# A stage multiplies its successor's first two projection lots before the border

## The chip, the cores and the metric

One core of a Trainium2 chip runs one program: two blocks, one after the other, each a row of stages. The metric is the device time of one execution in microseconds; the kernel before takes 3568.51 us at the median of three runs.

## The reference, cut to what matters

Each block computes, from the modulated and normed tokens `h` (256 context and 512 grid tokens, width 1024), projections through one large matrix, runs two recurrent mixers on them, gates and merges the two results and projects back:

```python
z = jnp.matmul(h, w_in)                                # all projections
oa, ob = mixer_a(z), mixer_b(z)                        # chunked scans, both directions
ya = rmsnorm(oa, ...) * silu(ag); yb = rmsnorm(ob, ...) * silu(bg)
gates = sigmoid(mg + b_gate)                           # mg is one of the projections
merged = gates[..., :D] * (ya @ w_a) + gates[..., D:] * (yb @ w_b)
out = merged @ w_o
```

In the first block mixer a is a gated linear attention (4 heads) and mixer b a gated delta network (4 heads). In the second, mixer a is HGRN2 (8 heads) and mixer b a state space mixer (8 groups), and a product-key expert layer follows. All is float32.

## The kernel before, in words

**Stages.** A stage is a function that gives each engine its own instruction stream inside one block; all engines meet in a barrier at its end, and PSUM and semaphores pass from one stage to the next only there. The four borders of this document lie between `gla_pairs` and `gdn_heads` (first block, mixers a and b), `gdn_heads` and `merge`, `gated_heads` and `ssd_groups` (second block, mixers a and b), `ssd_groups` and `merge`.

**Tiles and lots.** A mixer stage projects its weights tile by tile (128 output channels, 1024x128, 512 KB). SyncE loads tile n into one of two slots of the ring once `low_ready` says that the tile two before it was split; ScalarE casts it to a rounded high part (`high(n)`, after the matmuls that still read this slot: `lot_done`), and VectorE subtracts to get the low part (`low(n)`). TensorE multiplies a tile with the tokens in lots of 384 or 512 columns: a lot is 8 units (one for each 128 of the width), a unit is `product3`, three matmuls (low by high, high by low, high by high; lines 366 to 368). Lots go to PSUM banks 6 and 7 in turn, and ScalarE evicts them (`evict`, semaphore `evicted`).

**Fills.** The lots of a stage are one generator, `projection()`; `fill(count)` issues the next `count` units between the other TensorE work of a head, in an order written out by hand (`FILL`, `SLOT`). Each mixer works a head or group ahead, so in its last head or group the generator has run dry and the fills issue nothing. `onward` lists tiles of the successor: the stage loads and splits its successor's first two tiles (`ready` = 2 tells the successor so), but multiplies nothing with them.

**The ends.** `gla_pairs` handles two pairs of heads (steps `at` = 1 to 14 each): key rows (line 594) at step 9, state updates (608) at 8 and 10, output products (lines 638 and 641) at step 12, the sums of squares (648) at step 14, then ScalarE's rstd and VectorE's last product. In `gdn_heads` each head ends with six passes over the chunks: TensorE, VectorE, TensorE, VectorE, TensorE, VectorE, each waiting for the other (lines 1237, 1250, 1261 on TensorE; 1646, 1654, 1662 on VectorE), with the output products at 1269 and 1270 and `squares` (1189). `gated_heads` is built like `gla_pairs` with 8 heads (output products 3007 and 3010, squares 2962); in the last head bank 6 also turns the step sizes (line 3017), which ScalarE copies out (3147, `dt_kept`). `ssd_groups` has 8 steps in a group: ScalarE exponents, VectorE product (3826), TensorE output products (3554, 3555); the norm (3505) ends the last group, and then the stage waits for its store to DRAM.

**The starts.** `gdn_heads` forms running sums (1192), then `fill(24)` multiplies three lots; ScalarE evicts lot 0 once the convolution weights and the pair mask have landed (`const_in`), and VectorE begins with `low(2)` (line 1461) and the convolution of the queries. `ssd_groups` forms sums, then `fill(72)` multiplies all nine lots of the first group, the first four of 384 columns. `merge` multiplies 16 gate tiles (8 units of 512 columns each) in order into banks 0 to 7, the sigmoid evicts each (`gate_ready`); tile i+2 is split while tile i+1 is multiplied. Beside it, it loads the branch weights (0.5 MB in the first block, 1.5 MB in the second) and, in the second block, the mixer's result `yz` piece by piece.

## Time and profile before

| | |
|---|---|
| median of three runs | 3568.51 us (3567.75 to 3574.23) |
| profiled execution | 3568.87 us, span 3566.7 us, 48214 instructions |
| TensorE busy | 3304.1 us, 93% |
| VectorE, ScalarE, GpSimd busy | 2540.0, 1617.3, 547.7 us |
| `gla_pairs`' last output products to `gdn_heads`' first matmul | 259.9 to 270.0 us |
| `gdn_heads`' last output to merge's first matmul | 614.9 to 620.0 us |
| `gated_heads`' last output to `ssd_groups`' first lot | 1322.1 to 1335.4 us |
| `ssd_groups`' last output to merge's first matmul | 1921.4 to 1935.9 us |

The span is the time from the first to the last instruction that the profiler saw; the execution's own time lies 2.2 us above it. The lower four rows are the stretches around the borders in the timeline. Times in the timeline are microseconds from the start of the span. The engines are PE (TensorE), PEld (its weight loads), DVE (VectorE), ACT (ScalarE), POOL (GpSimd) and SP (SyncE); an engine name with a q is its instruction queue.

### The profile page before, as it was taken

The numbers are of one execution on the slowest core, as the hardware profiler recorded it, in microseconds if no ns is written. First come the engines' busy times: TensorE is split into PE (matmuls) and PEld (weight loads), VectorE is DVE, ScalarE is ACT, GpSimd is POOL, SyncE is SP. The second block draws the span as 40 slices with busy tenths as digits, with TensorE's granted clock in tenths as the row PEclk, the third lists the DMA queues.
The fourth block names the chain that finished last, engine by engine and source line by source line (L and its number), as shares of the span: only waits on it lengthen the run. The fifth ranks groups of instructions, "written<-read, shape, count | busy, mean of one in ns | idle before, by whom it ended". The sixth has DMA issues, their size and how long they took to land. (4 is left out here: it accounts for less than half of the span.)

```text
span 3566.7 us, 48214 instructions
## 1 busy us (share of the span) xinstructions
PE 3304.1 (93%) x18404; PEld 2877.1 (81%) x18404; DVE 2540.0 (71%) x4360; ACT 1617.3 (45%) x2671; POOL 547.7 (15%) x365
## 2 busy tenths in 40 slices
PE   7988998997999979999997998999998999999997
PEld 3867987875889878777875886899997788999996
DVE  2646886254877875887884435699995887888887
ACT  4433342325555543665564423433564444444444
POOL 0211010000433420000000000455100111222220
PEclk9989999998999989999998999999999999999999
DMA  5101110342111111111112324334467998999994
GB/s 222 36 24 54 31 36 20 117 166 95 46 50 48 48 30 55 48 54 48 60 48 94 108 89 193 140 134 150 149 216 274 359 355 329 354 354 354 345 355 158
DMA packets 152468, 521.20 MB, mean 146 GB/s; under 512 B 19136, under 2 KB 66096, under 8 KB 132400
## 3 DMA queue, kind: packets, MB, share of 16 engines
q1 hardware_dynamic: 133808, 383.90, 29.9%
q0 software_dynamic: 18432, 134.23, 10.2%
q8 instruction: 147, 2.41, 0.3%
q14 instruction: 81, 0.66, 0.1%
HBM read 474.01 MB, written 44.06 MB: 145 GB/s over the span
## 5 line engine op out<-in xcount | busy, mean ns | idle before, releaser
L366 PE MATMUL ps<-hT_high,ring_twin 128*128 128x384 f32 (+1 forms) x1768 | 691.3, 391 | 64.5 <-DVE ring_twin L3188 32.5
L368 PE MATMUL ps<-hT_high,ring_twin 128*128 128x384 f32 (+1 forms) x1768 | 649.9, 368 | 0.0
L367 PE MATMUL ps<-hT_low,ring_twin 128*128 128x384 f32 (+1 forms) x1696 | 621.5, 366 | 0.0
L366 PEld LDWEIGHTS ps<-hT_high,ring_twin 128*128 128x128 f32 x1768 | 343.8, 194 | 121.8 <-DVE ring_twin L3188 38.2
L368 PEld LDWEIGHTS ps<-hT_high,ring_twin 128*128 128x128 f32 x1768 | 342.4, 194 | 31.9
L367 PEld LDWEIGHTS ps<-hT_low,ring_twin 128*128 128x128 f32 x1696 | 330.4, 195 | 29.7 <-issue 2.9
L366 PE MATMUL ps<-ex_vh,ex_al 128*128 128x512 f32 x768 | 300.7, 392 | 18.7 <-DVE ex_al L2750 18.7
L2269 POOL TENSOR_TENSOR pr_wl<-pr_w,pr_wh 128x1024 fp32r<-128x1024 f32 x58 | 147.2, 2540 | 1040.3 <-ACT pr_wh L2328 1040.3
L368 PE MATMUL ps<-ex_vh,ex_ah 128*128 128x512 f32 x768 | 301.7, 393 | 0.0
L367 PE MATMUL ps<-ex_vl,ex_ah 128*128 128x512 f32 x768 | 301.6, 393 | 0.0
L2605 POOL DMA_INDIRECT ex_uv<-in_peer_uv,rows_at x128 | 169.9, 1327 | 806.4 <-DVE ex_acc L2709 566.7
L2660 ACT CAST ex_vh<-ex_v 128x1024 fp32r<-128x1024 f32 x128 | 134.1, 1048 | 159.3 <-PE ps L368 135.5
L2745 DVE TENSOR_TENSOR ex_vl<-ex_v,ex_vh 128x1024 fp32r<-128x1024 f32 x128 | 156.3, 1221 | 54.0 <-ACT ex_vh L2660 54.0
L366 PEld LDWEIGHTS ps<-ex_vh,ex_al 128*128 128x128 f32 x768 | 145.3, 189 | 49.3 <-DVE ex_vl L2745 15.2
L368 PE MATMUL ps<-ex_xh,ex_uh 128*128 128x384 f32 x512 | 171.9, 336 | 0.0
L366 PE MATMUL ps<-ex_xh,ex_ul 128*128 128x384 f32 x512 | 171.7, 335 | 0.0
L367 PE MATMUL ps<-ex_xl,ex_uh 128*128 128x384 f32 x512 | 171.5, 335 | 0.0
L368 PEld LDWEIGHTS ps<-ex_vh,ex_ah 128*128 128x128 f32 x768 | 145.1, 189 | 30.5
L367 PEld LDWEIGHTS ps<-ex_vl,ex_ah 128*128 128x128 f32 x768 | 145.1, 189 | 29.0
L2709 DVE SCALAR_TENSOR_TENSOR ex_acc<-ex_uv,ex_wts,ex_acc 128x1024 f32<-128x1024 f32 x127 | 162.5, 1280 | 3.8
L366 PE MATMUL ps<-ex_xh,pr_wl 128*128 128x384 f32 (+1 forms) x464 | 162.9, 351 | 1.1 <-POOL pr_wl L2269 1.1
L368 PE MATMUL ps<-ex_xh,pr_wh 128*128 128x384 f32 (+1 forms) x464 | 162.3, 350 | 0.0
(610 smaller groups left out, 7612.8 us busy)
## 6 DMA issues: line engine op xcount, KB each, us to landing
ex_v<-in_peer_uv SPq DMA_DIRECT2D x128, 512.0 KB
pr_w<-in_peer_u SPq DMA_DIRECT2D x64, 512.0 KB, 4.2
ex_u<-in_peer_u SPq DMA_DIRECT2D x64, 512.0 KB, 7.8
ring<-in_w_in_ma SPq DMA_DIRECT2D x48, 512.0 KB, 3.2
gates_by_expert<-sg_gbuf SPq DMA_DIRECT2D x6, 4096.0 KB, 14.7
ex_g<-gates_by_expert SPq DMA_DIRECT2D x32, 768.0 KB
ring<-in_w_in_hg SPq DMA_DIRECT2D x40, 512.0 KB, 3.2
ring<-in_w_merge SPq DMA_DIRECT2D x36, 512.0 KB, 3.6
```

The source lines that it names most:

```text
L366: pe.matmul(out, a[1], b[0], start=start, stop=False)
L367: pe.matmul(out, a[0], b[1], start=False, stop=False)
L368: return pe.matmul(out, a[0], b[0], start=False, stop=stop)
L2269: pool.tensor_tensor(wl[:, n % R, :], w[:, n % W, :], wh[:, n % R, :].bitcast(F32), ALU.subtract).then_inc(low_ready, 1)
L2605: pool.indirect_dma_start(uv[:, n % UV, :], None, d["peer_uv"], bass.IndirectOffsetOnAxis(ap=rows_at[:, n:n + 1], axis=0)).then_inc(uv_in[ ...
L2660: act.copy(vh[:, m % R, :], v[:, m % R, :]).then_inc(vh_ready, 1)
L2709: dve.scalar_tensor_tensor(out=acc[:], in0=uv[:, n % UV, D:2 * D], scalar=wts[:, n:n + 1], in1=acc[:], op0=ALU.mult, op1=ALU.add).then_inc ...
L2745: dve.tensor_tensor(vl[:, m % R, :], v[:, m % R, :], vh[:, m % R, :].bitcast(F32), ALU.subtract).then_inc(vl_ready, 1)
```

## The change

At each of the four borders the stage that ends gets a generator `leading()`, which multiplies the first two lots of its successor (tiles `len(tiles)` and `len(tiles) + 1` of the ring) into banks 6 and 7, and issues its 16 units between and behind the last head's own TensorE work with `lead(count)`. The successor raises `lot_done` (or `gate_done`) for these two lots instead of multiplying them, and its opening fill is 16 units shorter. For a merge as successor the stage also loads and splits two more gate tiles (four instead of two); the merge starts with gate tile 2, places gate i in bank (i + 6) % 8 and numbers its waits for `gate_ready` anew. The same lots, gates and results are computed.

```diff
@@ gla_pairs, TensorE (h is the last pair, steps 9 to 14)
+                def leading():
+                    for a, (n, t0, nt) in enumerate(((0, NCTX, NX), (1, 0, 384))):
+                        at = ring_at(len(tiles) + n)
+                        pe.wait_ge(low_ready, len(tiles) + n + 1)
+                        pe.wait_ge(evicted, len(lots) - 1 + a)
+                        for j in range(KD):
+                            c = slice(P * j, P * j + P)
+                            mm = product3(pe, ps[:, 6 + a, 0:nt], (wh[:, at, c], wl[:, at, c]),
+                                          (hT[0][:, j, t0:t0 + nt], hT[1][:, j, t0:t0 + nt]), j == 0, j == KD - 1)
+                            if j == KD - 1:
+                                mm.then_inc(lot_done, 1)
+                            yield
...
                         fill(FILL[at - 1])
+                        if h + 1 == H and at > 8:
+                            lead((4, 4, 4, 2, 2, 0)[at - 9])
@@ gdn_heads, projection(); the same in ssd_groups, whose fill(72) becomes fill(56)
+                            if m < 2:
+                                pe.sem_inc(lot_done, 1)
+                                m += 1
+                                continue
...
-                fill(24)
+                fill(8)
@@ gdn_heads, passes of the last head (leading() as above, both lots of 512 columns)
                             fill(3 if i == NC - 1 else 2)
+                        elif i > 0:
+                            lead(2)
+                lead(6)
                 squares(H - 1)
@@ gdn_heads, ScalarE and VectorE after the last head
+                high(tile_of(H, V))
                 squares(H - 1)
+                high(tile_of(H, G))
                 rstd(H - 1)
...
+                low(tile_of(H, V))
                 pre(H - 1)
+                low(tile_of(H, G))
                 tail(H - 1)
@@ gated_heads, TensorE (lots of 384 columns; the first also waits for dt_kept)
                         fill(FILL[at - 1])
+                        if h + 1 == H and at > 8:
+                            lead((3, 3, 3, 3, 2, 2)[at - 9])
@@ ssd_groups, TensorE, steps of the last group (lots of 512 columns)
                             rows_of(g, s + 2)
+                        if g + 1 == G and s > 1:
+                            lead(2)
...
+                lead(4)
                 norm(G - 1)
@@ ssd_groups, ScalarE and VectorE at the end
+                high(6 * G + 2)
                 squares(G - 1)
+                high(6 * G + 3)
                 rstd(G - 1)
...
+                low(6 * G + 2)
                 skipped(G - 1)
                 multiplied(G - 1)
+                low(6 * G + 3)
                 normed(G - 1)
@@ merge
+    READY, DONE = 4, 2
+    gate_bank = lambda i: (i + 6) % 8
...
                     sp.wait_ge(low_ready, i - 1)
-                    load_gate(i)
+                    if i >= READY:
+                        load_gate(i)
...
                 for i in range(GATES):
+                    if i < DONE:
+                        pe.sem_inc(gate_done, 1)
+                        continue
...
-                    if n < 4:
-                        pe.wait_ge(gate_ready, GATES - 6 + 2 * n)
-                    else:
+                    if n < 3:
+                        pe.wait_ge(gate_ready, GATES - 4 + 2 * n)
+                    elif n > 3:
                         pe.wait_ge(out_done, n - 3)
```

## Rows read from the trace of the kernel before

**Rows 1.** The page, TensorE's clock in 40 slices, in tenths of full speed

```profile
PEclk9989999998999989999998999999999999999999
```

**Rows 2.** The timeline of TensorE near 1345 and 1940 us (start, length, engine, line, operation)

```profile
1344.96 0.33 PE L366 MATMUL ps<-hT_high,ring_twin 128*128 128x384 f32 x1
...
1355.88 0.33 PE L366 MATMUL ps<-hT_high,ring_twin 128*128 128x384 f32 x1
...
1937.31 0.63 PE L366 MATMUL ps<-hT_high,ring_twin 128*128 128x512 f32 x1
...
1941.15 0.63 PE L366 MATMUL ps<-hT_high,ring_twin 128*128 128x512 f32 x1
...
1943.63 0.39 PE L366 MATMUL ps<-hT_high,ring_twin 128*128 128x512 f32 x1
...
1949.75 0.39 PE L366 MATMUL ps<-hT_high,ring_twin 128*128 128x512 f32 x1
```

**Rows 3.** Two windows, output products of both pairs: PE, PEld, DVE, ACT, POOL, clock, DMA

```profile
168.36:176.50 8.14, 8.14 (x48) 6.32 (x48) 8.11 (x6) 5.57 (x9) 4.32 (x3) 1.00 0.01 2
...
245.17:259.90 14.73, 14.72 (x48) 11.17 (x48) 0.99 (x1) 0.54 (x1) 0.00 (x0) 0.51 0.00 1
```

**Rows 4.** The timeline of gla_pairs' last steps; in brackets idle time and releaser

```profile
240.66 1.31 PE L608 MATMUL ps<-gla_vt,gla_ktok 128*64 128x128 f32 x20 [0.79 <-ACT gla_ktok L757]
...
245.17 0.46 PE L638 MATMUL ps<-gla_att,gla_vt 128*128 128x128 f32 x2 [3.20 <-DVE gla_S L875]
...
262.42 3.75 PE L648 MATMUL ps<-gla_scr,ones 128*128 128x512 f32 x4 [2.52 <-DVE yaT L935]
```

**Rows 5.** The timeline and the DMA view of gdn_heads' start

```profile
272.29 11.89 SPq L1039 DMA_DIRECT2D ring<-in_w_in_gdn  x3
...
281.05 1.05 ACT L1293 CAST ring_twin<-ring 128x1024 fp32r<-128x1024 f32 x1
...
282.13 1.69 DVE L1461 TENSOR_TENSOR ring_twin<-ring,ring_twin 128x1024 fp32r<-128x1024 f32 x1 [9.98 <-ACT ring_twin L1293]
...
ring<-in_w_in_gdn SPq DMA_DIRECT2D x4, 512.0 KB, 5.6
```

**Rows 6.** The timeline of gdn_heads' last passes and the merge's start

```profile
602.07 0.74 PE L1237 MATMUL ps<-gdn_S,gdn_k 128*128 128x128 f32 x4 [0.18 <-DVE gdn_S L1662]
...
605.35 0.61 PE L1237 MATMUL ps<-gdn_S,gdn_k 128*128 128x128 f32 x4
...
614.50 0.39 PE L1270 MATMUL ps<-gdn_att,gdn_vn 128*128 128x128 f32 x2
...
616.37 1.13 PE L1189 MATMUL ps<-gdn_scr,ones 128*128 128x512 f32 x2 [1.47 <-DVE ybT L1574]
...
620.00 0.50 PE L366 MATMUL ps<-hT_high,ring_twin 128*128 128x512 f32 x1 [2.51 <-DVEq L1887]
```

**Rows 7.** The timeline of gated_heads' end and ssd_groups' start

```profile
1315.64 0.48 ACT L3147 COPY rows<-ps 128x384 f32<-128x384 f32 x1 [5.59 <-PE ps L3017]
...
1317.70 0.77 PE L3007 MATMUL ps<-hg_att,hg_vt 128*128 128x128 f32 x2 [2.10 <-DVE hg_S L3254]
...
1323.65 1.10 PE L2962 MATMUL ps<-hg_scr,ones 128*128 128x512 f32 x2 [1.56 <-DVE oT L3265]
...
1335.38 0.69 PE L366 MATMUL ps<-hT_high,ring_twin 128*128 128x384 f32 x1 [2.71 <-DVEq L3742]
...
1348.18 1.23 DVE L3745 TENSOR_TENSOR ring_twin<-ring,ring_twin 128x1024 fp32r<-128x1024 f32 x1 [12.94 <-ACT ring_twin L3580]
```

**Rows 8.** Windows and timeline of ssd_groups' end and the second merge's start

```profile
1911.30:1921.40 10.10, 6.53 (x52) 5.14 (x52) 2.45 (x2) 6.67 (x14) 0.00 (x0) 0.50 0.00 0
1935.90:1942.00 6.10, 6.10 (x14) 4.76 (x15) 0.00 (x0) 0.00 (x0) 0.00 (x0) 0.50 0.87 315
...
1926.08 3.78 PE L3505 MATMUL ps<-ma_y,ones 128*128 128x512 f32 x4 [4.67 <-ACT ma_y L3650]
...
1944.69 1.05 ACT L1806 CAST ring_twin<-ring 128x1024 fp32r<-128x1024 f32 x1 [13.44 <-DMA ring<-in_w_merge]
```

More of the change, by code:

```diff
@@ L535, in fill, with lead @@
                         next(ahead, None)
+                def leading():
[10 more added lines that the diff above has]
+                            yield
+                leads = leading()
+                def lead(count):
+                    for _ in range(count):
+                        next(leads, None)
                 def rates(h, dr, bank):
@@ L1000, in gdn_heads @@
         lots = [(n, t0, nt, t0 - parts[0][0]) for n, (_, parts) in enumerate(tiles) for t0, nt in parts]
-        first_lot = [next(m for m, lot in enumerate(lots) if lot[0] == n) for n in range(len(tiles))] + [len(lots)]
+        first_lot = [next(m for m, lot in enumerate(lots) if lot[0] == n) for n in range(len(tiles))] + [len(lots), len(lots) + 1, len(lots) + 2]
         tile_of = lambda h, what: 4 * h + what
@@ L1103, in fill, with leading, lead @@
                         next(ahead, None)
+                def leading():
+                    for a, (n, t0, nt) in enumerate(((0, NCTX, NX), (1, NCTX, NX))):
+                        at = ring_at(len(tiles) + n)
+                        pe.wait_ge(low_ready, len(tiles) + n + 1)
+                        pe.wait_ge(evicted, len(lots) - 1 + a)
+                        for j in range(KD):
+                            c = slice(P * j, P * j + P)
+                            mm = product3(pe, ps[:, 6 + a, 0:nt], (wh[:, at, c], wl[:, at, c]),
+                                          (hT[0][:, j, t0:t0 + nt], hT[1][:, j, t0:t0 + nt]), j == 0, j == KD - 1)
+                            if j == KD - 1:
+                                mm.then_inc(lot_done, 1)
+                            yield
+                leads = leading()
+                def lead(count):
+                    for _ in range(count):
+                        next(leads, None)
                 def rates(h, lot):
@@ L1411, in _ @@
                         if lv == 0:
-                            high(tile_of(h + 1, V))
+                            if more:
+                                high(tile_of(h + 1, V))
                             if h > 0:
@@ L1430, in _ @@
                             value_rows(h, 1)
-                            high(tile_of(h + 1, G))
+                            if more:
+                                high(tile_of(h + 1, G))
                         if lv == 4 and more:
@@ L1800, in gate_high @@
                 def gate_high(i):
-                    if i < 2:
+                    if i < READY:
                         act.sem_inc(high_ready, 1)
                     else:
-                        act.wait_ge(g_in[i % 2], 16 * (i // 2))
+                        act.wait_ge(g_in[i % 2], 16 * (i // 2 - READY // 2 + 1))
                         act.wait_ge(gate_done, i - 1)
@@ L1811, in gate @@
                     act.wait_ge(gate_done, i + 1)
-                    act.activation(mixed_f[:, a, n, :], ps[:, i % 8, :], ACT.Sigmoid, **kw).then_inc(gate_ready, 1)
+                    act.activation(mixed_f[:, a, n, :], ps[:, gate_bank(i), :], ACT.Sigmoid, **kw).then_inc(gate_ready, 1)
                 def branch_high(n):
@@ L1885, in _ @@
                     dve.wait_ge(high_ready, i + 1)
-                    if i < 2:
+                    if i < READY:
                         dve.sem_inc(low_ready, 1)
@@ L2119, in first_block @@
         gdn_heads(core, k, hT, gates, b_rows, m1, ybT, 2, 0,
-                  [d["w_merge"][0][:, 8 + KD * n:8 + KD * n + KD, :] for n in range(2)])
+                  [d["w_merge"][i // 2][:, 8 + KD * (i % 2):8 + KD * (i % 2) + KD, :] for i in range(4)])
         tap("ybT", ybT[:])
@@ L2938, in fill, with leading, lead @@
                         next(ahead, None)
+                def leading():
+                    for a, (n, t0, nt) in enumerate(((0, 0, 384), (0, 384, 384))):
+                        at = ring_at(len(tiles) + n)
+                        pe.wait_ge(low_ready, len(tiles) + n + 1)
+                        pe.wait_ge(evicted, len(lots) - 1 + a)
+                        if a == 0:
+                            pe.wait_ge(dt_kept, 1)
+                        for j in range(KD):
+                            c = slice(P * j, P * j + P)
+                            mm = product3(pe, ps[:, 6 + a, 0:nt], (wh[:, at, c], wl[:, at, c]),
+                                          (hT[0][:, j, t0:t0 + nt], hT[1][:, j, t0:t0 + nt]), j == 0, j == KD - 1)
+                            if j == KD - 1:
+                                mm.then_inc(lot_done, 1)
+                            yield
+                leads = leading()
+                def lead(count):
+                    for _ in range(count):
+                        next(leads, None)
                 fill(72)
@@ L3381, in ssd_groups @@
         lots = [(n, t0, nt, dst, t0 - parts[0][0]) for n, (_, parts, dst) in enumerate(tiles) for t0, nt in parts]
-        first_lot = [next(m for m, lot in enumerate(lots) if lot[0] == n) for n in range(len(tiles))] + [len(lots)]
+        first_lot = [next(m for m, lot in enumerate(lots) if lot[0] == n) for n in range(len(tiles))] + [len(lots), len(lots) + 1, len(lots) + 2]
         lots_to = lambda g, what: first_lot[6 * g + what + 1]
@@ L3432, in projection @@
                         for t0, nt in parts:
+                            if m < 2:
+                                pe.sem_inc(lot_done, 1)
+                                m += 1
+                                continue
                             if m >= 2:
@@ L3447, in fill, with leading, lead @@
                         next(ahead, None)
+                def leading():
+                    for a, (n, t0, nt) in enumerate(((0, NCTX, NX), (1, NCTX, NX))):
+                        at = ring_at(len(tiles) + n)
+                        pe.wait_ge(low_ready, len(tiles) + n + 1)
+                        pe.wait_ge(evicted, len(lots) - 1 + a)
+                        for j in range(KD):
+                            c = slice(P * j, P * j + P)
+                            mm = product3(pe, ps[:, 6 + a, 0:nt], (wh[:, at, c], wl[:, at, c]),
+                                          (hT[0][:, j, t0:t0 + nt], hT[1][:, j, t0:t0 + nt]), j == 0, j == KD - 1)
+                            if j == KD - 1:
+                                mm.then_inc(lot_done, 1)
+                            yield
+                leads = leading()
+                def lead(count):
+                    for _ in range(count):
+                        next(leads, None)
                 def turned(g, src, half):
@@ L3508, in _ @@
                 sums(0)
-                fill(72)
+                fill(56)
                 for src in range(2):
@@ L3890, in _ @@
                             timed(g, 1)
-                        if s in (1, 3, 5, 7):
+                        if not last and s in (1, 3, 5, 7):
                             low(n + (B, C, Z0, Z1)[(1, 3, 5, 7).index(s)])
@@ L3929, in mixer_block @@
                 ssd_groups(core, k, hT, dt, loga, yz_dram, 2, 1,
-                           [d["w_merge_2"][0][:, 24 + KD * n:24 + KD * n + KD, :] for n in range(2)])
+                           [d["w_merge_2"][i // 2][:, 24 + KD * (i % 2):24 + KD * (i % 2) + KD, :] for i in range(4)])
             yzT, yz_low = core.twin(ctx2, "yzT", [P, 2 * MA_GROUPS, NX], F32, F32R)
```

2 lines of the change are left out of this document (1 added, 1 removed).

## The prediction, made before the changed kernel ran

> **What bounds the kernel now.** I read the page first. Its clock line [rows 1] stands at 8 or 9 tenths in only a few slices, and TensorE is busy 93% of the span; the dips lie where one stage ends and the next begins, because every stage closes with a barrier. So a microsecond of TensorE there counts only if TensorE is what the border waits for. The timelines of the four borders then say who sets the time: near 270 us (gla_pairs to gdn_heads), 620 (gdn_heads to merge), 1327 (gated_heads to ssd_groups), 1933 (ssd_groups to merge). What comes after a border depends on nothing but its own start, so I add up four borders.
>
> One unit of a lot is three matmuls. At the full granted clock (1.0, 2.4 GHz) 384-column matmuls follow each other every 10.92 / 63 = 0.173 us, 512-column ones every 6.12 / 27 = 0.227 us; at the half clock (1.2 GHz) a 512-column one takes 3.84 / 9 = 0.427 us, a 384-column one then about 0.32 us (estimate, three quarters of that) [rows 2].
>
> **Part 1, gla_pairs to gdn_heads: its tail.** In the last pair no fills are left. TensorE stood 3.2 us idle before the output products at 245.17 and about 0.8 us before that; then the 48 output products took 14.7 us at granted clock 0.51, where the pair before did the same 48 in 8.1 us at 1.00, filled up to the start [rows 3]. The leads at steps 9 to 11 are 8 units of 512 and 4 of 384: 24 x 0.227 + 12 x 0.173 = 7.5 us, of which 4.0 fill the idle time, so the products start 3.5 us later. With no gap ahead of them I take them at full clock: minus 6.6. The four units of steps 12 and 13 (2.1 us) fit into the 2.5 us before the sums at 262.42, and these (3.75 us at half clock) take half: minus 1.9 [rows 4]. Tail: 3.5 - 6.6 - 1.9 = minus 5.0 us; bounds minus 5.0 and, with the half clock staying for the products and sums, plus 3.5.
>
> **Its start.** gdn_heads is not led by TensorE but by VectorE's chain of convolutions, and this opens with the low part of tile 2 at 282.13, for which VectorE waited 10.0 us on the ScalarE cast at 281.05, which waits for lot 0. With lots 0 and 1 there, the cast waits for its load instead: issued at 272.29, 5.6 us to landing, so 277.9. Minus 3.2 us. That is all this border can give here, although 16 units (9.6 us) leave it: the third lot, which now comes first, waits for the eviction of lot 0, and that for the convolution weights and the pair mask, and has time until the chain needs it. Bounds 0 and minus 5. [rows 5]
>
> Of the moved low(2) one thing speaks against the gain: at 282.13 it took 1.69 us where GpSimd ran beside it, against 1.23 us for the same operation at 1348.18 [rows 5, 7]. The Trainium skill (SBUF — State Buffer, "SBUF: two separate sides") says that VectorE and GpSimd lock a shared pair of ports for a whole instruction. By that rule an earlier low(2) meets more of GpSimd's opening work. The rule would make the total some 0.5 us smaller; the sum leaves it in the bounds.
>
> **Part 2, gdn_heads to merge.** In the last head TensorE and VectorE pass each chunk back and forth. At pass 1 TensorE stood only 0.2 us idle before its next product (602.07), from pass 2 on none (605.35 starts right behind the output products). lead(2) is 6 x 0.227 = 1.36 us: passes 1 to 4 cost 1.1 + 3 x 1.36 = 5.2 us on the chain. After the output products end (614.9) come lead(2) and lead(6), 24 x 0.227 = 5.4 us, ahead of squares, which used to start at 616.37: plus 4.0. The two new casts and low parts lie in ScalarE's idle stretch (it does nothing in these passes) and beside the sums: 0. Their two loads on SyncE's queue go behind those of tiles 16 and 17, once that slot's low part is done, in the head before, and ahead of growth(3), which waits for the end of that head anyway: 0. (ssd_groups likewise loads two more tiles in its last group, ahead of its last two stores; these wait for out_ready.) Tail plus 9.2 us [rows 6]. In return the merge starts with gate 2: TensorE is back to back from 620.00 on, so 2 x 24 x 0.227 = 10.9 us go (at the half clock that starts there, the remaining gates now pay the same). Net minus 1.7; bounds plus 9.2 - 10.9 - 1.7 = minus 3.4 if the stage no longer drops to half clock, and plus 2 if the drop lasts twice as long. Waits for gate_ready are re-numbered, but all but the last gates are evicted long before.
>
> **Part 3, gated_heads to ssd_groups.** The first three lead units (9 x 0.173 = 1.56 us) wait for dt_kept at 1316.12 and just fill the 1.6 us until the output products at 1317.70. The other 13 (39 x 0.173 = 6.8 us) lie ahead of squares, which had 1.6 us of idle: plus 5.2. The products and their gap were 4.3 us long; if the clock stays full I give them 1.5 us back (less than the ratio of [rows 3], since part of them was at full clock already). Tail plus 3.7; bounds 3.3 and 5.5. The start is TensorE's: VectorE waited 12.94 us for the cast of tile 2, behind lots 0 and 1, and both lots go: 48 x 0.173 = 8.3 us at full clock (the half-clock stretch at the start I take to fall on the lots that follow, with the same loss). The next lot must wait for an eviction of 0.5 us that can only start at 1335.4 and VectorE's next tile for its load (3 to 4 us after 1335.4, hidden): plus 0.6. Net 3.7 - 7.7 = minus 4.0; bounds 0 and minus 6 [rows 7].
>
> **Part 4, ssd_groups to merge.** Between 1911.3 and 1921.4 TensorE was busy 6.5 of 10.1 us, at clock 0.50, while ScalarE's exponents set the pace; then 4.7 us idle before the sums at 1926.08. The leads after steps 2 to 6 fill such gaps and should cost 0.3 to 0.6 us in two steps; the last six units (18 x 0.227 = 4.1 us) fit into the 4.7 us. In return the sums (3.78 us at half clock) may run at the full one, minus 1.9. I take minus 1.2, between minus 1.9 and plus 1.5. Two casts and low parts lie in ScalarE's and VectorE's waits there. The merge again loses 10.9 us of gates. Its first load of a gate, which ScalarE used to get after 13.44 us of waiting, now has 1.5 MB of branch weights and two pieces of yz ahead of it, but is needed only after two gates as before (low part by some 11 to 13 us after the start). Net minus 12.1; bounds minus 14 and minus 5 [rows 8].
>
> **Sum.** -8.2 - 1.7 - 4.0 - 12.1 = -26.0 us. The profiled execution took 3568.87 us, 2.2 more than its span of 3566.7, and is 0.4 above the median of the three runs, 3568.51. 3568.87 - 26.0 = 3542.9, at the median 3542.5 us. Two runs of one kernel agree to about 0.2% (7.1 us), which is what a measurement here can tell from no change.
>
> **The rivals.**
> *Loads set the starts* (12%). In gdn_heads and ssd_groups the loads issued only after the barrier lead instead of TensorE, so that neither start gives anything: -26.0 + 3.2 + 7.7 = -15.1, 3553.4 us. For it: the 5.6 us loads of [rows 5]. Against: in ssd_groups VectorE's 12.94 us of waiting stood on TensorE's lots.
> *TensorE arrives warm* (13%). If the leads keep the clock full across the border, the half-clock stretch at the start of the successors goes too. At 1935.9 to 1942.0 it was 6.1 us, in which TensorE did 14 matmuls that take 3.2 us at 0.227: 2.9 us less. Three such starts, one of them shorter, give some 7 us: 3535.5 us. Against: between the last sums and the next stage 3 to 6 us without TensorE work remain. The Trainium skill (TensorE: Matmul & The Clock Gate, "What's actually happening") puts it that the throttled state is the default and activity releases it; by that rule the leads could do just this, and the trace agrees for the 48 products of [rows 3].
> *The merge starves* (8%). Gate 4 of the second merge lands late behind 2.5 MB, and one gate's time (5.4 us) is lost: 3548 us. For it: a wait of 13.44 us for a load there [rows 8].
> *Longer tails* (12%). The leads in the recurrences cost twice what I give parts 2 and 3 (another 9.2 + 3.7 = 12.9 us), since TensorE executes in order and every late product makes VectorE late: 3555.4 us.
> *The leads run at half clock* (5%), and the kernel is slower. Then the tails are: part 1, 24 x 0.427 + 12 x 0.32 = 14.1, less 4.0, plus 10.1, and its gain of 8.5 is gone; part 2, 2.4 + 3 x 2.56 + 10.2 - 1.5 = 18.8; part 3, 48 x 0.32 = 15.4 less 3.2 = 12.2; part 4, 48 x 0.427 = 20.5 less about 12.5 us of idle = 8.0. Sum plus 49.1, less 32.7 for the starts: plus 16.4, 3584.9 us. It decides from where about 60% of the 192 lead matmuls run at half clock (26.0 of the 42.4 us between the two sums). Against: three of the four tails begin at clock 1.0 and the leads close the gaps.
>
> My forecast has 50%, with a range of its own of 3538 to 3548. The range 3534 to 3557 takes in warm starts and longer tails and leaves out the slow case and the edges: about 2 in 10. Faster by over 0.2% (below 3561.4) 88%: all but the last rival, less 7% for two of the dear cases at once, which would land within 0.2%; slower 5%.
>
> **What the changed profile would show.** Part 1: output products of the last pair at clock 1.0 and some 8 us long; gdn_heads' first convolution about 3 us nearer to its start, with ScalarE waiting for a load. Part 2: passes 1 to 4 longer by 1.1 to 1.4 us each, squares 5.4 us behind the last output product, and 14 gates in the merge. Part 3: squares some 7 us behind the products, VectorE's first wait in ssd_groups short and on a load. Part 4: no later end of the last step, sums of 1.9 us, and TensorE back to back through 14 gates. Wrong would be: output products at half clock, TensorE waiting for gate 4, or a start whose first VectorE operation does not come earlier.

## The result, and the profile after

The changed kernel takes 3540.73 us at the median of four runs (3539.29 to 3544.83), the kernel before beside it 3568.18: ratio 0.9921, 95% interval 0.9904 to 0.9938. The forecast was 3542.5. The profiled execution, on which the readings below rest, was the longest of the four: 3544.83 us, span 3542.7, against 3568.87 and 3566.7.

To find where the time went I take the same VectorE operation in both timelines and follow how much earlier (minus) it comes after than before. A stretch is worth the change of this offset across it:

| stretch | forecast | measured | offset at its end |
|---|---|---|---|
| ahead of any changed code (to 242 us) | 0 | +2.6 | +2.6 |
| gla_pairs' tail | -5.0 | -4.5 | -1.9 |
| gdn_heads' start | -3.2 | -1.9 | -3.8 |
| gdn_heads' passes and tail | +9.2 | +9.0 | +5.2 |
| first merge | -10.9 | -12.3 | -7.1 |
| gated_heads' tail | +3.7 | +3.6 | -3.6 |
| ssd_groups' start | -7.7 | -8.1 | -11.7 |
| ssd_groups' first groups | 0 | -2.7 | -14.4 |
| ssd_groups' tail | -1.2 | +0.6 | -13.7 |
| second merge | -10.9 | -11.0 | -24.7 |
| all behind it | 0 | +0.6 | -24.0 |

Nine of the eleven are within 2.0 us of the forecast; the two others are stretches in which nothing was changed. The last digits come from one profile each and vary (see the first experiment). The page's clock line answers to [rows 1]: the dip of the 22nd slice, where ssd_groups ends, is gone; the others stay (one has moved from the 3rd to the 4th slice).

```profile
PEclk9998999998999989999999999999999999999999
```

The windows of the profile after (PE, PEld, DVE, ACT, POOL, clock, DMA) answer to [rows 3, 8]. gla_pairs' output products run at clock 1.00, not 0.51; the first merge's gates too; the second merge still starts at half clock.

```profile
251.37:259.72 8.35, 8.35 (x50) 6.41 (x49) 0.00 (x0) 0.00 (x0) 0.00 (x0) 1.00 0.00 0
625.40:642.00 16.60, 16.60 (x73) 13.76 (x74) 2.45 (x2) 5.71 (x7) 0.00 (x0) 1.00 0.47 159
1921.00:1926.00 5.00, 3.59 (x9) 2.82 (x10) 0.00 (x0) 2.37 (x3) 0.00 (x0) 0.51 0.62 203
```

The timeline after, gla_pairs' end and gdn_heads' start, answers to [rows 4, 5]:

```profile
251.37 0.38 PE L657 MATMUL ps<-gla_att,gla_vt 128*128 128x128 f32 x2
...
262.31 1.96 PE L667 MATMUL ps<-gla_scr,ones 128*128 128x512 f32 x4 [0.22 <-DVE yaT L956]
...
272.54 0.59 ACT L1362 COPY gdn_raw<-ps 128x512 f32<-128x512 f32 x1 [1.19 <-DMA gdn_pair<-in_pair_mask]
...
275.00 1.04 ACT L1341 CAST ring_twin<-ring 128x1024 fp32r<-128x1024 f32 x1 [1.28 <-DMA ring<-in_w_in_gdn]
275.02 7.54 POOL L1085 TENSOR_TENSOR gdn_TU<-ident,gates 128x768 f32<-128x768 f32 x4
...
276.08 1.50 DVE L1513 TENSOR_TENSOR ring_twin<-ring,ring_twin 128x1024 fp32r<-128x1024 f32 x1 [6.48 <-ACT ring_twin L1341]
...
277.51 11.44 DVE L1540 SCALAR_TENSOR_TENSOR gdn_q<-gdn_raw,gdn_cw,gdn_q 128x441 f32<-128x441 f32 x8
```

The products no longer have idle time ahead of them, and the sums take 1.96 us where they took 3.75. Behind the border ScalarE waits for a load, as forecast, and the low part of tile 2 (line 1513) starts 6.05 us earlier than before. But the first convolution (line 1540) takes 11.44 us; before it took 5.81, since GpSimd's diagonals (line 1085, until 282.74) were over when it began. Now they run beside it until 282.56, and GpSimd's next two products, which before fell on the second low part and the operation behind it, run beside it too. Before, and then after:

```profile
276.93 5.81 POOL L1064 TENSOR_TENSOR gdn_TU<-ident,gates 128x768 f32<-128x768 f32 x4
...
291.10 4.23 POOL L1058 TENSOR_TENSOR rows<-gdn_strict,gates 128x768 f32<-128x768 f32 x2 [8.36 <-PE ps L1116]
291.49 2.50 DVE L1461 TENSOR_TENSOR ring_twin<-ring,ring_twin 128x1024 fp32r<-128x1024 f32 x1
```

```profile
283.60 3.44 POOL L1079 TENSOR_TENSOR rows<-gdn_strict,gates 128x768 f32<-128x768 f32 x2 [1.03 <-PE ps L1161]
```

Of the eight operations of this convolution (441 to 504 columns each) five took 1.78 to 1.89 us, three beside the diagonals and two beside line 1079; each of the five began while a product of GpSimd was running. The other three took 0.68 to 0.74 us, as all eight did before.

gdn_heads' last passes and the first merge, answering to [rows 6]:

```profile
599.33 0.61 PE L1282 MATMUL ps<-gdn_S,gdn_k 128*128 128x128 f32 x4
...
603.90 0.61 PE L1282 MATMUL ps<-gdn_S,gdn_k 128*128 128x128 f32 x4
...
621.49 1.02 PE L1234 MATMUL ps<-gdn_scr,ones 128*128 128x512 f32 x2
625.39 0.50 PE L366 MATMUL ps<-hT_high,ring_twin 128*128 128x512 f32 x1 [2.88 <-DVEq L1949]
```

A pass is now 4.57 us long, where 602.07 to 605.35 was 3.28: plus 1.29. By VectorE's operations the four passes with leads make plus 5.1 us, where 5.2 was forecast. gated_heads' end and ssd_groups' start, answering to [rows 7]:

```profile
1309.04 0.41 PE L366 MATMUL ps<-hT_high,ring_twin 128*128 128x384 f32 x1 [0.66 <-ACT rows L3232]
...
1310.68 0.38 PE L3090 MATMUL ps<-hg_att,hg_vt 128*128 128x128 f32 x2
...
1320.12 1.02 PE L3045 MATMUL ps<-hg_scr,ones 128*128 128x512 f32 x2
...
1335.05 1.04 ACT L3692 CAST ring_twin<-ring 128x1024 fp32r<-128x1024 f32 x1 [2.32 <-DMA ring<-in_w_in_ma]
1336.12 1.23 DVE L3859 TENSOR_TENSOR ring_twin<-ring,ring_twin 128x1024 fp32r<-128x1024 f32 x1 [4.47 <-ACT ring_twin L3692]
```

The first three lead units fill the gap ahead of the products, the sums come 6.8 us behind them, and VectorE's wait at the start is 4.47 us instead of 12.94, behind a load. Last ssd_groups' end, answering to [rows 8]:

```profile
1906.05 0.80 PE L366 MATMUL ps<-hT_high,ring_twin 128*128 128x512 f32 x1
...
1908.25 0.20 PEld L3663 LDWEIGHTS ps<-ma_decay,ma_xdt 128*64 128x64 f32 x4 [0.37 <-issue]
...
1914.20 1.98 PE L3614 MATMUL ps<-ma_y,ones 128*128 128x512 f32 x4 [0.50 <-ACT ma_y L3762]
...
1922.41 0.80 PE L366 MATMUL ps<-hT_high,ring_twin 128*128 128x512 f32 x1 [6.22 <-DVEq L1949]
```

The sums run in 1.98 us instead of 3.78. But the two units behind step 6 stand ahead of the last output products and take 2.2 us, the first three of their six matmuls at half clock; before, TensorE stood 0.15 us idle there.

### The profile page after: what moved, and what is told of

It is laid out like the page before. It is cut to its first block and busy times, and to the rows that moved or that the text cites. A ratio compares the mean times of both kernels' runs of the same rounds, so it can differ in the third digit from the quotient of the medians.

```text
span 3542.7 us, 48233 instructions
## 1 busy us (share of the span) xinstructions
PE 3289.7 (93%) x18404; PEld 2867.9 (81%) x18404; DVE 2542.8 (72%) x4360; ACT 1617.8 (46%) x2671; POOL 555.1 (16%) x365
```

## The experiments

Twelve runs: the changed kernel once more, nine kernels with one edit each and two that combine edits. Medians go with the changed kernel's 3540.8 us (median of its nine executions, 3538.95 to 3544.83); ratios are to the kernel before. Where I speak of the trace, it is the offset to the profile of after, as above, across one stretch.

### The changed kernel again

No edit.

> The changed kernel once more, as it is. Theory: the drift of about 2.5 us between 50 and 130 us in the profile of after, ahead of all changed code, is that execution's own (it was the longest of its four) and the median is 3540.7 us within 2 us; before 80 us the profile has the same number of stretches at half clock as the other runs' or one fewer than in the first profile. Rival: the change has moved something there (code or data placed elsewhere), and the drift is found again.

3540.82 us (3538.95 to 3542.07), ratio 0.9918 (0.9904 to 0.9931). At 242 us it is 2.4 us earlier than the first profile: that drift belonged to the one execution. It is also the yardstick for what a single profile can tell: from the first profile to the repeat 1.2 us are gained in ssd_groups' last group (between 1850 and 1895 us), 1.1 us in the second merge, and 0.5 us are lost behind it. All other rows of the table but the first come out within 0.5 us.

### Without the gdn_heads to merge border

```diff
-                        elif i > 0:
-                            lead(2)
-                lead(6)
...
-    READY, DONE = 4, 2
+    READY, DONE = (2, 0) if b_dram is None else (4, 2)
```

> The changed kernel without its part 2: gdn_heads multiplies and loads nothing more for the merge, and the first merge multiplies all 16 gates; the three other borders as changed. Theory: part 2 was worth about 3.1 us (in the profiles of before and after the stage pair changed by +9.0 and -12.1), of which 1.2 to 1.6 us is clock, since the leads keep TensorE busy until the border. Then the passes are 3.3 us apart again, the merge starts with a stretch at half clock (some 8 matmuls 0.43 us apart), and the span is 3545.8 us. Rival: the merge's full clock in the profile of after was chance; then the merge starts at clock 1.0 here too and the span is about 3544.2 us.

3545.70 us (3543.36 to 3548.34), ratio 0.9938 (0.9922 to 0.9955). From the first pass to the merge's later gates it is 3.3 us longer than after. The timeline of its first merge:

```profile
613.50 0.63 PE L366 MATMUL ps<-hT_high,ring_twin 128*128 128x512 f32 x1
...
616.06 0.63 PE L366 MATMUL ps<-hT_high,ring_twin 128*128 128x512 f32 x1
617.09 0.39 PE L366 MATMUL ps<-hT_high,ring_twin 128*128 128x512 f32 x1
```

Six matmuls take 2.56 us, 0.43 each, before the clock is full again: without the leads the half clock is back, as it was in the kernel before. The rival as I put it fails, but the theory is not shown either. Of the twelve profiles in which the leads run up to this merge, eight start it at full clock. In four, all of kernels below (gla_pairs' leads late, GpSimd's diagonals later, and the two that combine edits), it has a stretch at half clock all the same, and is 1.4 to 1.6 us longer, although TensorE stood 2.88 us idle before it in all twelve; the first two of these kernels don't touch the leads here at all. The windows of the merge's start, in after and then with the diagonals later:

```profile
625.40:637.00 11.60, 11.60 (x51) 9.62 (x52) 1.22 (x1) 4.38 (x6) 0.00 (x0) 1.00 0.54 183
617.10:628.70 11.60, 11.60 (x44) 9.44 (x45) 1.23 (x1) 4.03 (x5) 0.00 (x0) 0.85 0.44 149
```

Part 2 therefore buys 1.7 us, as forecast, and in eight profiles of twelve 1.6 us more as clock. What decides between the two is open.

### gla_pairs' leads behind the products

```diff
-                            lead((4, 4, 4, 2, 2, 0)[at - 9])
+                            lead((0, 0, 0, 8, 8, 0)[at - 9])
```

> The changed kernel, with all 16 units of gla_pairs' leads behind the last output products instead of 12 ahead of them and 4 behind. Theory: the idle time ahead of the products is what costs them the clock. Then the products start 3.5 us earlier than in after but take about 14.7 us at half clock instead of 8.1, and the sums of squares start 10 us later than in after (leads at full clock) to 17 us later (leads at half clock). Rival: the clock has nothing to do with the gap; then the products take 8.1 us, the leads 9.6, and the sums start 3.5 us later.

3555.21 us (3550.12 to 3560.04), ratio 0.9964 (0.9950 to 0.9978). Its timeline:

```profile
244.25 0.46 PE L657 MATMUL ps<-gla_att,gla_vt 128*128 128x128 f32 x2 [3.20 <-DVE gla_S L896]
...
258.90 0.79 PE L366 MATMUL ps<-hT_high,ring_twin 128*128 128x512 f32 x1
...
270.00 1.88 PE L667 MATMUL ps<-gla_scr,ones 128*128 128x512 f32 x4
```

The gap of 3.20 us is back and the products take 14.65 us. The stage ends 11.1 us later than in after, with the same lots: the products start 3.6 us earlier but take 6.3 us more, and the 16 units between them and the sums, the first two still at half clock, take 8.5 us more than four did. So the place of the leads is worth more than the leads: 12 units in the idle time keep the clock for what follows. Here the profiles leave no exception: in all twelve with leads ahead of these products they run at clock 1.00, in the two without (this one and the kernel before) at 0.51.

### GpSimd's diagonals later, or on VectorE

```diff
@@ one kernel
                 rates(0)
+                pool.wait_ge(sig_ready, 2)
                 diagonal(0, 0, t_init)
@@ the other: the four diagonals as dve.tensor_tensor, ahead of low(0)
```

> The changed kernel, where GpSimd's four opening diagonals in gdn_heads wait for the sigmoid of the keys. Theory: the first convolution took 11.4 us instead of 5.8 because it ran beside them. Then its 8 operations take 5.8 us, the diagonals are 5.8 to 7.5 us somewhere behind 290, the operations of VectorE that they then run beside are longer, and the later work of gdn_heads is 2 to 5.6 us earlier than in after. Rival: the convolution is slow for another reason (half clock of TensorE, the landing weights); then it keeps 11.4 us and nothing moves.

> The changed kernel, with the four opening diagonals of gdn_heads done by VectorE in the 6.5 us in which it waited for the cast of tile 2. Theory (shared cost of GpSimd beside VectorE): four operations of about 1.0 us, up to 2 us each where GpSimd's rates run beside; GpSimd is done at about 7.5 us from the stage's start, tile 2's low part starts where it did or at most 1.5 us later, the convolution takes 5.8 us, and the later work of gdn_heads is 4 to 5.6 us earlier than in after. Rival: the convolution keeps 11.4 us, and the later work is later by what the diagonals delay the low part.

Later: 3538.32 us (3535.98 to 3540.99), ratio 0.9913 (0.9897 to 0.9930). On VectorE: 3538.72 us (3537.90 to 3539.44), ratio 0.9917 (0.9900 to 0.9933). The timeline of the first:

```profile
275.52 5.81 DVE L1541 SCALAR_TENSOR_TENSOR gdn_q<-gdn_raw,gdn_cw,gdn_q 128x441 f32<-128x441 f32 x8
...
291.58 6.92 POOL L1085 TENSOR_TENSOR gdn_TU<-ident,gates 128x768 f32<-128x768 f32 x4 [18.92 <-ACT gdn_sg L1374]
...
294.77 2.40 DVE L1527 SCALAR_TENSOR_TENSOR gdn_v<-gdn_raw,gdn_cw,gdn_v 128x255 f32<-128x255 f32 x2 [2.28 <-ACT gdn_v L1364]
297.20 5.41 DVE L1541 SCALAR_TENSOR_TENSOR gdn_v<-gdn_raw,gdn_cw,gdn_v 128x441 f32<-128x441 f32 x3
```

The convolution of the queries is back at 5.81 us, and the operations that now run beside GpSimd's products (the diagonals until 298.50, line 1079 until 302.13) are the long ones: 2.40 us for two that took 1.00 to 1.01, 5.41 for three that took 2.11. There they cost less, because VectorE had waits to lose: from the end of gla_pairs to the first level 6.0 us are won, a little more than the 5.6 expected at most. On VectorE the diagonals take 4.08 us in the idle time and the convolution 5.80, but both low parts now meet GpSimd's other work (1.89 and 2.50 us), and 3.7 us are won, less than the 4 expected at least. The theory stands, its rival falls. The medians show only 2.5 and 2.1 us of it, which spreads of 1.5 to 6 us don't resolve. In the profiles part of the gain is lost again in code that the edits don't touch: with the later diagonals 1.6 us in the first merge, and 2.0 and 2.6 us behind the second.

### The leads of gdn_heads into the levels

```diff
                                 squares(h - 1)
                                 fill(2)
+                                if h + 1 == H:
+                                    lead(2)
...
                         if lv < 6:
                             fill(2)
+                        if lv < 2 and h + 1 == H:
+                            lead(2)
...
-                        elif i > 0:
-                            lead(2)
-                lead(6)
+                lead(10)
```

> The changed kernel, with the leads of gdn_heads elsewhere: 2 units while TensorE waits for the rstd of the head before (1.4 us idle in the profile of after), 2 behind each of the first two levels of the last head (1.1 and 1.4 us idle), none in the passes, 10 behind the last output products. Theory: a lead unit in the passes or behind the products costs its full 0.68 us, one in idle time nothing. Then the passes are 3.3 us apart, the levels take at most 0.5 us longer, and the end of the stage comes 3.6 to 4.1 us earlier than in after. Rival: every unit delays the chain wherever it stands, because TensorE hands each level on as late as it works; then the end comes at most 1 us earlier.

3540.16 us (3538.52 to 3543.60), ratio 0.9923 (0.9907 to 0.9940). Passes and sums in its timeline:

```profile
602.35 0.61 PE L1286 MATMUL ps<-gdn_S,gdn_k 128*128 128x128 f32 x4
605.53 0.61 PE L1286 MATMUL ps<-gdn_S,gdn_k 128*128 128x128 f32 x4
...
615.38 1.02 PE L1234 MATMUL ps<-gdn_scr,ones 128*128 128x512 f32 x2
```

Passes are 3.18 us apart again, the levels take no longer, and the stage ends 3.7 us earlier: six units in idle time cost nothing. In the median 0.6 us are left.

### gated_heads: bank 7's lot into the gaps

```diff
-                    for a, (n, t0, nt) in enumerate(((0, 0, 384), (0, 384, 384))):
+                    for a, n, t0, nt in ((1, 0, 384, 384), (0, 0, 0, 384)):
...
-                        if h + 1 == H and at > 8:
-                            lead((3, 3, 3, 3, 2, 2)[at - 9])
+                        if h + 1 == H and at > 3:
+                            lead((4, 3, 1, 0, 0, 3, 3, 0, 0, 0, 0)[at - 4])
                 squares(H - 1)
+                lead(2)
```

> The changed kernel, with gated_heads' second lead lot (bank 7, which waits for no step size) first: 4 units behind step 4, 3 behind step 5, 1 behind step 6 of the last head, where TensorE stood 2.4 and 1.55 us idle; then the first lot, 3 units each at steps 9 and 10, and 2 behind the sums of squares. Theory: these 8 units are free there and the 2 behind the sums as well, and what runs between them keeps the full clock; the end of the stage comes 5 us earlier than in after by the units alone and up to 8 with the clock. Rival: the last head's levels wait for GpSimd and ScalarE and not for the clock, and the leads wait in order for the eviction of bank 7; then the end comes 3 us earlier or less.

3538.28 us (3537.43 to 3544.13), ratio 0.9921 (0.9904 to 0.9937). Its timeline, the last level products and the sums:

```profile
1295.56 1.13 PE L3039 MATMUL ps<-hg_mix 128*128 128x128 f32 x8 [0.31 <-DVE hg_mix L3319]
...
1300.45 1.13 PE L3039 MATMUL ps<-hg_mix 128*128 128x128 f32 x8 [1.51 <-DVE hg_mix L3319]
...
1311.55 1.10 PE L3045 MATMUL ps<-hg_scr,ones 128*128 128x512 f32 x2 [0.20 <-DVE oT L3351]
```

The level products take 1.1 us each, where after's of the same steps took 2.05. The stage ends 6.0 us earlier. But 2.9 us come back in the first group of ssd_groups. Half of it (1.6 us) lies ahead of the second group, where the kernel before and this one have a half-clock stretch that after has not. The window of the kernel before:

```profile
1470.00:1480.00 10.00, 8.10 (x40) 6.50 (x39) 4.37 (x4) 5.26 (x11) 0.00 (x0) 0.83 0.01 2
```

The same work in after, 13 matmuls more in 10 us:

```profile
1456.00:1466.00 10.00, 8.10 (x53) 6.38 (x51) 5.39 (x6) 5.27 (x11) 0.00 (x0) 1.00 0.01 2
```

And in this kernel:

```profile
1450.00:1460.00 10.00, 8.10 (x46) 6.72 (x45) 4.62 (x5) 5.27 (x11) 0.00 (x0) 0.83 0.01 2
```

This accounts for 1.6 of the 2.7 us of the table that nobody forecast. The other 1.1 us (here 1.4) arise some 90 us earlier, between 1370 and 1400 us of the profile of after. There all three kernels have a stretch at half clock, in after 2 to 3 us earlier against the work; that this is the cause is not shown. The stretch ahead of the second group is there in the kernel before, here and in both combined kernels, and absent in the other ten profiles.

### ssd_groups: no lead ahead of the last products

```diff
-                            lead(2)
+                            lead((2, 2, 2, 5, 0, 0)[s - 2])
...
-                lead(4)
+                lead(5)
```

> The changed kernel, with the leads in the last group of ssd_groups after steps 2 to 7 as 2, 2, 2, 5, 0, 0 and 5 at the end, in place of 2 after each and 4 at the end. Theory: the two units after step 6 ran at half clock ahead of the last output products and cost 1.7 us of tail, where the 2.5 us of idle time before step 6's products was left open. Then the end of the stage comes 1.5 to 2.2 us earlier than in after. Rival: the clock falls in ScalarE's wait all the same and the fifth unit of that step delays its products; then it comes less than 0.5 us earlier.

3540.71 us (3538.19 to 3543.93), ratio 0.9921 (0.9905 to 0.9938). The last two steps' products:

```profile
1904.62 0.45 PE L3663 MATMUL ps<-ma_decay,ma_xdt 128*64 128x128 f32 x4 [0.43 <-DVE ma_decay L3940]
...
1906.79 0.45 PE L3663 MATMUL ps<-ma_decay,ma_xdt 128*64 128x128 f32 x4 [1.03 <-DVE ma_decay L3940]
```

They run at full clock, and the tail is 1.9 us shorter than in after. The 1.2 us that the second profile of the unedited kernel had by itself lie elsewhere, between 1850 and 1895 us. Across the last steps (1908 to 1918 us in after) the offset moves by 2.0 us here and by 2.0 and 1.9 us in the two kernels below that have this edit too, and by no more than 0.1 us in the nine runs without it, the repeat among them. So the trace bears the theory out at 2.0 us. The median shows nothing of it (3540.71 against 3540.8), which a spread of 5.7 us doesn't resolve.

### One lot only to gdn_heads

```diff
-                    for a, (n, t0, nt) in enumerate(((0, NCTX, NX), (1, 0, 384))):
+                    for a, (n, t0, nt) in enumerate(((0, NCTX, NX),)):
...
-                            lead((4, 4, 4, 2, 2, 0)[at - 9])
+                            lead((3, 3, 2, 0, 0, 0)[at - 9])
...
-                fill(8)
+                fill(16)
```

> The changed kernel, but gla_pairs multiplies only the first lot of gdn_heads (8 units, 3, 3 and 2 behind steps 9 to 11), and gdn_heads multiplies the second in its opening fill. Theory: gdn_heads' start waits for lot 0 alone, and 8 units are enough to keep TensorE's clock ahead of the output products. Then the products start 2.1 us earlier than in after and take 8.1 us, and gla_pairs ends about 2 us earlier; the first convolution starts as late behind the border as in after. Rival: with half the units the clock falls (products up to 14.7 us), or the second lot is missed at the start, and its 4.2 us come back there: then gdn_heads' chain is 2 us later than in after, or more.

3542.84 us (3540.56 to 3544.56), ratio 0.9922 (0.9907 to 0.9938). Its timeline:

```profile
249.68 0.38 PE L657 MATMUL ps<-gla_att,gla_vt 128*128 128x128 f32 x2
...
260.62 3.75 PE L667 MATMUL ps<-gla_scr,ones 128*128 128x512 f32 x4 [2.52 <-DVE yaT L956]
```

The products start 2.1 us earlier and keep the full clock, so eight units are enough for that; and the second lot is not missed at the start. But now nothing stands behind the products, the sums are at half clock again (3.75 us), and of 2.1 us only 0.3 are left at the end of the stage. My expectation of 2 us was wrong: it had left out the four units behind the products.

### Products without use ahead of the second merge

```diff
                 norm(G - 1)
+                for _ in range(4):
+                    pe.matmul(ps[:, 3, :], k.ones[:], y[:, 0, :], start=True, stop=True)
```

> The changed kernel, with four products of 512 columns behind the last sums of squares of ssd_groups, written to a bank that nobody reads any more: 3.8 us of TensorE work without use in the 6.2 us before the second merge. Theory: the merge starts at half clock because TensorE stood idle before it (the first merge starts at full clock behind 2.9 us, the second at half clock behind 6.2). Then the gates go at 0.227 us a matmul from the first on and the second merge is 2.6 us shorter than in after. Rival: the idle time is not what decides, or 2.4 us left are enough to lose the clock; then some 13 matmuls still go at 0.43 us and nothing is gained.

3540.02 us (3539.80 to 3540.76), ratio 0.9916 (0.9901 to 0.9931). Its timeline:

```profile
1912.15 3.60 PE L3680 MATMUL ps<-ma_y,ones 128*128 128x512 f32 x8
...
1918.53 0.50 PE L366 MATMUL ps<-hT_high,ring_twin 128*128 128x512 f32 x1 [2.78 <-DVEq L1949]
...
1930.91 0.50 PE L366 MATMUL ps<-hT_high,ring_twin 128*128 128x512 f32 x1 [1.17 <-DVE ring_twin L1952]
```

The merge starts at full clock: from its start on 48 matmuls in 11.5 us, where after had 40 in 11.6, so 8 x 0.227 = 1.8 us are won. Then TensorE stands 1.17 us idle at the third gate it multiplies, for its low part, which waited for its load. The gate's load had been hidden only because TensorE was slow. What is left is 1.1 us against after, less than half of the 2.6 expected. Even that can't be put down to the products: the repeat and the kernels without part 2, with one lot only and with gated_heads' leads in the gaps have none, and gain 1.0 to 1.2 us in the same stretch. Nor do the products ensure the clock, as the last kernel shows.

### Together

The diagonals later and the three other placements of leads; then the same with one lot only and the products without use.

> The changed kernel with the later diagonals, and the leads of gdn_heads, gated_heads and ssd_groups placed as in the three runs before. Theory: the gains add up: 6.0 (measured between the ends of gla_pairs and the first level of gdn_heads), 3.8, 6 and 1.7 us, 17.5 in all: 3523 us, 3518 to 3530. Rival: a gain in one place comes back as half clock in the next, and no more than half is left: 3532 us.

> The kernel of the run called best, with one lot led to gdn_heads and the four products without use behind ssd_groups. Theory: another 2.0 and 2.6 us on top of 3525.8 us: 3521 us. Rival: either fails by its rival above, 3524 us or more.

The first: 3525.80 us (3518.34 to 3527.78), ratio 0.9873 (0.9857 to 0.9890), 15.0 us below the changed kernel, faster than both in every execution and within the 3518 to 3530 us expected. The second: 3529.31 us (3526.57 to 3532.67), ratio 0.9890 (0.9874 to 0.9905): its additions bring nothing that can be measured. In the trace of the first, the four places give 4.4, 3.7, 6.0 and 3.1 us (1.2 of the last as in the repeat, without an edit); 1.4 us come back in the first merge and 3.0 in ssd_groups' first group. In the trace of the second TensorE again stands only 2.78 us idle between the products without use and the second merge, and this time the merge starts at half clock:

```profile
1897.72 3.60 PE L3684 MATMUL ps<-ma_y,ones 128*128 128x512 f32 x8
1904.10 0.80 PE L366 MATMUL ps<-hT_high,ring_twin 128*128 128x512 f32 x1 [2.78 <-DVEq L1952]
...
1905.54 0.63 PE L366 MATMUL ps<-hT_high,ring_twin 128*128 128x512 f32 x1
```

## Why the prediction was right, point by point

**Part 1, tail.** Right in each term: products 3.6 us later by the units (3.5 forecast), 6.4 us shorter at full clock (6.6), sums 1.8 us shorter (1.9). The late leads show that the clock term hangs on the gap: with the gap back the products take 6.3 us more. The rest of those 11.1 us are units that no longer fill idle time.

**Part 1, start.** The release was right (the cast waits for its load), the term was mis-sized, 1.9 us where 3.2 was written. The step that failed is "the sum leaves it in the bounds": I priced the meeting with GpSimd at 0.5 us. Against the end of gla_pairs the low part came 4.2 us earlier (6.05 less 1.9), more than the 3.2 of the forecast. The low part itself was 0.2 us shorter than before. The first convolution then lost 5.6 us, 3.3 of them beside the diagonals and 2.2 beside line 1079; and 2.5 us came back at tile 3's low part and the operation behind it, which line 1079 had met before. A wait that became 0.6 us shorter makes up the rest of the 1.9. So line 1079 only changed whom it slows; what the forecast lacked is the 3.3 us of the diagonals. The Trainium skill (SBUF — State Buffer, "SBUF: two separate sides") has the two engines lock a shared port pair. The delayed diagonals agree: the long operations (1.78 us for one of 0.68) are in each case ones beside a product of GpSimd.

**Part 2.** The tail was right to 0.2 us: a unit in a chain that TensorE leads costs its full time. The merge gave 1.4 us more in this profile, because it has no half-clock stretch at its start, so that part 2 comes to minus 3.3: the forecast's own bound of minus 3.4 "if the stage no longer drops to half clock". That is a piece of the rival *TensorE arrives warm*, on one of three starts. In this profile the text's "the remaining gates now pay the same" fails; in the four profiles that keep the stretch it holds, and with a merge 1.6 us longer part 2 is worth the minus 1.7 of the forecast. So this gain is in part luck.

**Part 3.** Right in both terms, with the marks it named.

**Part 4.** The merge was right; it did not starve. The tail came out at plus 0.6 instead of minus 1.2: the forecast let every unit but two fit into waits, and the pair behind step 6 took 2.2 us, in part at half clock, ahead of the last products. The gain of the sums (1.8 us) was as forecast. With the pair elsewhere (the experiment on ssd_groups) the last steps are 2.0 us shorter. The size of the miss is less sure: in the repeat's profile the tail is minus 0.4.

**The rest.** The four borders make minus 24.6 us in the profile, the forecast minus 26.0. The profile's other terms (+2.6, -2.7, +0.6) lie in code that is the same in both kernels. The first belongs to one execution; the second is looked at in the experiment on gated_heads; the third was not followed up. The median fell by 27.4 us, which is the borders and the 2.7 us together. So the premise "What comes after a border depends on nothing but its own start" failed, and the median lies within 1.8 us of the forecast partly by luck: borders that gave 1.4 us too little met 2.7 us that nobody had forecast. Without these and without the 1.4 us of the first merge it would be some 3545 us by my estimate, still inside the range. One row was misread, without effect on the sum: the clock line of [rows 1] stands at 8 or 9 tenths in all slices and at 8 in four, not "in only a few slices" at 8 or 9.

**The rivals.** Loads set both mixer starts, as the first rival said, but behind the gain, not in place of it. The merge did starve once it was made faster. The half-clock leads did not come: all but a handful of units ran at the full clock.

## What to carry to other kernels

Moving work of TensorE across a border pays only where it lands in idle time; in a chain that TensorE leads, each unit costs what it saves later. Place it ahead of long TensorE work that follows a gap: there it also keeps the clock, which here (8.2 us in the products and sums) was worth more than the moved work. When an operation moves earlier, list what other engines do at its new time, GpSimd beside VectorE above all, and price it from a row where the two met. Before a full or half clock in one profile is put down to the change, look at the same stretch in the profiles of the other kernels that share its code.

## What the runs showed of the hardware

- VectorE beside GpSimd lost more than half its speed: a convolution operation of 441 columns that began while GpSimd ran a product of 768 columns took 1.78 to 1.89 us, alone 0.68. GpSimd's product took 1.56 to 2.46 us there, alone 1.48, and its four diagonals 7.54 us instead of 5.81.
- The 48 output products of gla_pairs ran at clock 1.00 in all twelve profiles with leads ahead of them and at 0.51 in both profiles with a gap of 3.20 us there.
- The first merge, behind 2.9 us without TensorE work when the leads ran up to it, had no half-clock stretch in eight profiles and one that cost 1.4 to 1.6 us in four. Without the leads, behind 2.5 us, it had one in both profiles. The second started at half clock in all twelve profiles in which TensorE stood 6.0 to 6.2 us idle before it. When 3.6 us of these held products without use, it started at full clock in one kernel and at half clock in the other. The Trainium skill (TensorE: Matmul & The Clock Gate, "What's actually happening") has activity release a throttled default. The output products agree; the starts of the merges agree only in part, since they differ behind the same idle time.
- Stretches at half clock also come and go in code that was not changed. A loss of 2.7 to 3.0 us in ssd_groups' first group, with one such stretch in it, was there in the kernel before, absent in after and its repeat, and there again in all three kernels with gated_heads' leads in the gaps. A gain of 2 to 6 us in one stage can be half gone at the end for no reason in that stage; what sets the place of these stretches stays open.
